# Two transformer blocks in one kernel: rotations of the woven attention cut into slices, and four copies and read-outs put elsewhere in their engines' order

## What is computed

```python
def first_block(x, mem, ...):
    ...
        h = h + memory_cross_attention(rms_norm(h, xattn_norm_g[i]), memn, w_q[i], w_k[i], w_v[i], w_xo[i])
        h = h + swiglu(rms_norm(h, ffn_norm_g[i]), w_gate[i], w_up[i], w_down[i])

def second_block(x, ...):            # two layers
        yA = forgetting_attention(heads(qA), heads(kA), heads(vA), fA, forget_bias[l])      # "fox"
        yB = dsa_attention(rope(heads(qB), pos), rope(kB, pos), vB, rope(qI), rope(kI), wI) # "dsa"
        r = retention(rope(heads(qC), pos), rope(heads(kC), pos) * HEAD_DIM ** -0.5, heads(vC))
        yC = head_groupnorm(r, ret_norm[l]) * jax.nn.silu(gC)
        yD = sliding_window_gqa(rope(heads(qD), pos), rope(heads(kD), pos), heads(vD), attn_sinks[l])  # "swa"
        branch = jnp.einsum('bsnc,ncd->bsnd', ys, w_branch[l])
        merged = jnp.sum(jax.nn.sigmoid(gates) * branch, axis=2)
        x = x + merged @ w_out[l]
        u = causal_dwconv(rmsnorm(x, ffn_norm[l]) @ w_up[l], conv_w[l], conv_b[l])
        a, b = jnp.split(u, 2, axis=-1)
        x = x + (jax.nn.silu(a) * b) @ w_down[l]
```

## Time and profile before

| | |
|---|---|
| median of three runs | 3037.11 us (3036.61 to 3038.03) |
| the profiled execution | 3039.78 us, its span 3037.8 us |
| PE busy | 2988.0 us (98%) |
| DVE, ACT, POOL busy | 1391.3, 1289.9, 1398.2 us (46%, 42%, 46%) |
| granted TensorE clock, mean | 0.997 |
| chain that ended last | PE 89%, DVE 6%, ACT 2%, POOL 1% |
| first woven attention, layer 0 and 1 | about 1085 to 1258 and 2122 to 2295 us |

### The profile page before, as it was taken

The page is one execution under the profiler, slowest core; times in us unless marked ns, Lnnn a source line. Parts: engine busy times, 40 slices in busy tenths (PEclk is TensorE's granted clock), DMA queues, the critical chain, the costliest instruction groups (busy, mean ns, idle before and its releaser), DMA issues.

```text
span 3037.8 us, 39928 instructions
## 1 busy us (share of the span) xinstructions
PE 2988.0 (98%) x15302; PEld 2438.1 (80%) x15302; DVE 1391.3 (46%) x2189; ACT 1289.9 (42%) x2219; POOL 1398.2 (46%) x1002
## 2 busy tenths in 40 slices
PE   8999999999999999999999999999999999999998
PEld 7778887788888777878888888878787788878887
DVE  7874351421113878562116433168776520264322
ACT  5443443433333446554234444244564533354432
POOL 5345574444444543234455454554332354544543
PEclk9999999999999999999999999999999999999999
DMA  5234242233333423223333333244231233333332
GB/s 158 83 112 144 87 132 91 77 97 97 99 97 85 142 69 89 53 67 87 97 93 99 94 97 99 83 109 138 68 91 42 64 98 97 97 94 97 97 97 71
DMA packets 214891, 287.61 MB, mean 95 GB/s; under 512 B 42682, under 2 KB 122610, under 8 KB 213042
## 3 DMA queue, kind: packets, MB, share of 16 engines
q1 hardware_dynamic: 212210, 279.88, 31.5%
q0 software_dynamic: 880, 2.99, 0.3%
q10 hardware_dynamic: 1616, 2.23, 0.2%
HBM read 269.80 MB, written 4.72 MB: 90 GB/s over the span
## 4 chain that ended last, share of the span: by engine, by line
PE 89%; DVE 6%; ACT 2%; POOL 1%; issue 1%; DMA 0%; ACTq 0%; SPq 0%; DVEq 0%
PE half L732 80%; PE half L1169 1%; PE half L1155 1%; PE half L1226 1%; POOL wL L2917 1%; PE half L1138 1%; PE half L1133 1%; DVE arena L2082 1%; DVE arena L2681 1%; DVE arena L2715 1%; PE half L987 0%; PE half L1004 0%; DVE rms L2073 0%; PE half L1212 0%; DVE arena L2706 0%
## 5 line engine op out<-in xcount | busy, mean ns | idle before, releaser
L2917 POOL TENSOR_TENSOR wL<-slot,wH 128x512 fp32r<-128x512 f32 (+1 forms) x976 | 1366.5, 1407 | 1610.1 <-ACT wH L1336 1609.0
L1336 ACT ACTIVATE wH<-slot 128x512 fp32r<-128x512 f32 (+1 forms) x976 | 603.4, 625 | 1229.3 <-PE half L732 1223.7
L732 PE MATMUL half<-nH,wH 128*128 128x512 f32 x2336 | 922.6, 395 | 8.1 <-POOL wL L2917 3.1
L732 PE MATMUL half<-nH,wL 128*128 128x512 f32 x2336 | 910.2, 390 | 0.0
L732 PE MATMUL half<-nL,wH 128*128 128x512 f32 x2336 | 909.7, 389 | 0.0
L732 PE MATMUL half<-arena_split,wH 128*128 128x512 f32 (+1 forms) x2432 | 735.8, 385 | 1.7 <-issue 0.8
L732 PEld LDWEIGHTS half<-nH,wH 128*128 128x128 f32 x2336 | 438.5, 188 | 119.7 <-issue 20.2
L732 PEld LDWEIGHTS half<-arena_split,wH 128*128 128x128 f32 x2432 | 451.2, 188 | 94.6 <-issue 3.4
L732 PEld LDWEIGHTS half<-nH,wL 128*128 128x128 f32 x2336 | 438.5, 188 | 92.6
L732 PEld LDWEIGHTS half<-nL,wH 128*128 128x128 f32 x2336 | 438.8, 188 | 89.2 <-issue 1.4
L732 PE MATMUL half<-arena_split,wL 128*128 128x512 f32 (+1 forms) x1216 | 466.4, 384 | 0.0
(11 more groups left out here) (351 smaller groups left out, 2656.5 us busy)
## 6 DMA issues: line engine op xcount, KB each, us to landing
slot<-in_w_in SPq DMA_DIRECT2D x344, 256.0 KB, 2.7
slot<-in_w_up SPq DMA_DIRECT2D x440, 128.0 KB, 2.2
slot<-in_w_down SPq DMA_DIRECT2D x132, 256.0 KB, 2.6
slot<-in_w_branch SPq DMA_DIRECT2D x64, 256.0 KB, 2.6
slot<-in_w_out SPq DMA_DIRECT2D x48, 256.0 KB, 2.8
slot<-in_w_gate SPq DMA_DIRECT2D x88, 128.0 KB, 2.1
arena<-arena SPq DMA_DIRECT2D x40, 256.0 KB, 4.4
slot<-in_w_proj_b SPq DMA_DIRECT2D x16, 256.0 KB, 2.9
```

The lines of the kernel that those rows point to most:

```text
L732: mm = pe.matmul(dst, lhsT, rhs, start=(k == 0 and m == 0), stop=(k == last and m == 2))
L1336: act.activation(wH[:, p, 0:cols], slot[:, s, 0:cols], ACT.Copy).then_inc(weights_high, 1)
L2917: pool.tensor_tensor(wL[:, p, 0:cols], slot[:, s, 0:cols], plainly(wH[:, p, 0:cols]), ALU.subtract)\
```

## The change

1. **Rotations.** Every rotation is cut into twelve instructions of 128x512 (`rope_slices`): four times sin, four times cos, four sums. A table says how many are done after which iteration (count in brackets): qB after -1, 0, 1, 2 (3 each); qC after 4 (1), 5 (1), 6 (2), 7 (2), 8 (1), 9 (1), 10 (2), 11 (2); kC after 13 (1), 14 (2), 15 (1), 16 (2), 17 (2), 18 (2), 20 (2); qD after 24 (2), 25 (2), 26 (2), 27 (3), 28 (3). None is left inside an iteration.
2. **Stacks.** `STACK_AT` goes from (9, 11, 17, 21) to (11, 14, 18, 22).
3. **First block, copy of the queries.** The last unit of `awq1` on PE signals after its first two banks, and ACT copies these two before it waits for the unit's end.
4. **Read-outs of gates 1 and 2.** ACT reads the first bank right after the last unit, ahead of the copy of the turn, and the other three where all four were read.
5. **Retention gate.** DVE does it in iteration 1 of `WEAVE_S` between `negated` and `inverse`, and not after `normed`.
6. **Feed-forward.** Units 4 and 5 of `bup2` are rounded by ACT around the first group's silu and rounding, and only 6 and 7 after `conv_last(1)`.

```diff
-STACK_AT = (9, 11, 17, 21)
+STACK_AT = (11, 14, 18, 22)
...
-                    unit(ps[1], "awq1", k, stream)
+                    if k < KD - 1:
+                        unit(ps[1], "awq1", k, stream)
+                    else:
+                        unit(ps[1], "awq1", k, stream, part=[0, 1]).then_inc(S["bank_done"], 1)
+                        unit(ps[1], "awq1", k, stream, part=[2, 3]).then_inc(weights_used, 1)
...
+            act.wait_ge(S["bank_done"], 1)
+            act.activation(xq[:, 4:6, :], banks(1)[:, 0:2, :], ACT.Copy).then_inc(S["xq_read"], 1)
             done(act, "awq1")
-            act.activation(xq[:, 4:6, :], banks(1)[:, 0:2, :], ACT.Copy).then_inc(S["xq_read"], 1)
...
+                    for n in (1, 2):
+                        if (f"bgt{n}a", KD - 1) in weave.at(it):
+                            done(act, f"bgt{n}a", l)
+                            if n == 1:
+                                read_out(act, "btC", l)
+                            else:
+                                act.wait_ge(S["yc_split"], l + 1)
+                            evac_by_bank(gate_b[n], jobs.half[f"bgt{n}a"], part=[0])
                     if weave.has(it):
                         turned(s, False)
...
-                    if 0 < g < NG - 1:
+                    if g == 1:
+                        round_units("bup2", l, 0, [6, 7], 512)
+                    elif 0 < g < NG - 1:
                         others(f"bup{g + 1}", l)
...
                     act.activation(conv[:, p, 0:2, :], conv[:, p, 0:2, :], ACT.Silu).then_inc(S["silu"], 1)
+                    if g == 0:
+                        round_units("bup2", l, 0, [4], 512)
                     act.wait_ge(S["ff_ready"], l * NG + g + 1)
                     round_ff(conv[:, p, 0:2, :], g)
+                    if g == 0:
+                        round_units("bup2", l, 0, [5], 512)
...
+                def rope_slices(name, buf, n, first, count):
+
+                    if first == 0:
+                        dve.wait_ge(S["partners"], l * 320 + 64 * n + 64)
+                        read_out(dve, name, l)
+                    for at in range(first, first + count):
+                        op, j = divmod(at, NB)
+                        if op == 0:
+                            link(dve.tensor_tensor(part[:, j, :], part[:, j, :], C["sin"], ALU.mult))
+                        elif op == 1:
+                            link(dve.tensor_tensor(buf[:, j, :], buf[:, j, :], C["cos"], ALU.mult))
+                        else:
+                            ins = dve.tensor_tensor(buf[:, j, :], buf[:, j, :], part[:, j, :], ALU.add)
+                            if j == NB - 1:
+                                ins.then_inc(S["roped"], 1)
...
                     if amid:
-                        rope(*amid)
+                        amid()
...
-                pieces = {0: ("bqB", qB, 1, [0]), 1: ("bqB", qB, 1, [1]), 3: ("bqB", qB, 1, [2]),
...
-                    woven(WEAVE_A, it, ("bqC", qC, 2, [0]) if it == 6 else None)
-                    if it in pieces:
-                        rope(*pieces[it])
+                    woven(WEAVE_A, it)
+                    for name, buf, n, taken in turned_by:
+                        if it in taken:
+                            rope_slices(name, buf, n, sum(taken[x] for x in taken if x < it), taken[it])
                     if it - 1 in STACK_AT:
...
-                    woven(WEAVE_S, it)
+                    woven(WEAVE_S, it, retained_gated if it == TURN_C else None)
```

More of the change, by code:

```diff
@@ L1344, in others, with evac_by_bank @@
                 round_units(name, l, i, range(SPLITS, ring.units[name]), cols)
-            def evac_by_bank(to, h, func=ACT.Copy, **kw):
-                for j in range(4):
+            def evac_by_bank(to, h, func=ACT.Copy, part=range(4), **kw):
+                for j in part:
                     ins = act.activation(to[:, j, :], ps[h][:, j * T:j * T + T], func, **kw)
@@ L1951, in gate_read @@
                         read_out(act, gates_used[n - 3], l)
-                    elif n == 1:
-                        read_out(act, "btC", l)
-                    elif n == 2:
-                        act.wait_ge(S["yc_split"], l + 1)
                     h = jobs.half[name]
                     if n < 3:
-                        evac_by_bank(gate_b[n], h)
+                        evac_by_bank(gate_b[n], h, part=range(1, 4) if n else range(4))
                     else:
@@ L2755, in _ @@
                 dve.wait_ge(S["forget_rows"], 16 * PAIRS * (l + 1))
-                pieces = {0: ("bqB", qB, 1, [0]), 1: ("bqB", qB, 1, [1]), 3: ("bqB", qB, 1, [2]),
-                          7: ("bqC", qC, 2, [1]), 9: ("bqC", qC, 2, [2]),
-                          13: ("bkC", kC, 3, [0]), 15: ("bkC", kC, 3, [1]), 17: ("bkC", kC, 3, [2]),
-                          26: ("bqD", qD, 4, [0]), 27: ("bqD", qD, 4, [1]), 28: ("bqD", qD, 4, [2])}
+                turned_by = [("bqB", qB, 1, {-1: 3, 0: 3, 1: 3, 2: 3}),
+                             ("bqC", qC, 2, {4: 1, 5: 1, 6: 2, 7: 2, 8: 1, 9: 1, 10: 2, 11: 2}),
+                             ("bkC", kC, 3, {13: 1, 14: 2, 15: 1, 16: 2, 17: 2, 18: 2, 20: 2}),
+                             ("bqD", qD, 4, {24: 2, 25: 2, 26: 2, 27: 3, 28: 3})]
                 def weigh_retained(i):
@@ L2792, in _, with retained_gated @@
                 dve.tensor_tensor(grouped, grouped, wide(mean, HD), ALU.subtract).then_inc(S["group_centred"], 1)
+                def retained_gated():
+                    dve.wait_ge(S["gc_ready"], l + 1)
+                    dve.wait_ge(S["y_turned"], l + 1)
+                    h = jobs.half["btC"]
+                    for c in range(NB):
+                        ins = dve.scalar_tensor_tensor(out=gC[:, c, :], in0=ps[h][:, c * T:c * T + T],
+                                                       scalar=vec[:, W_RET + c:W_RET + c + 1], in1=gC[:, c, :],
+                                                       op0=ALU.mult, op1=ALU.mult)
+                        if c < 3:
+                            ins.then_inc(S["bank_read"], 1)
+                    ins.then_inc(S["yc_ready"], 1)
+                    dve.wait_ge(S["yc_ready"], l + 1)
+                    dve.sem_inc(drained[h], 1)
                 for it in WEAVE_S.its:
-                    woven(WEAVE_S, it)
+                    woven(WEAVE_S, it, retained_gated if it == TURN_C else None)
                     if it == -AHEAD:
@@ L2801, in _ @@
                         dve.tensor_tensor(grouped, grouped, wide(mean, HD), ALU.mult).then_inc(S["group_normed"], 1)
-                    if it == TURN_C:
-                        dve.wait_ge(S["gc_ready"], l + 1)
-                        dve.wait_ge(S["y_turned"], l + 1)
-                        h = jobs.half["btC"]
-                        for c in range(NB):
-                            ins = dve.scalar_tensor_tensor(out=gC[:, c, :], in0=ps[h][:, c * T:c * T + T],
-                                                           scalar=vec[:, W_RET + c:W_RET + c + 1], in1=gC[:, c, :],
-                                                           op0=ALU.mult, op1=ALU.mult)
-                            if c < 3:
-                                ins.then_inc(S["bank_read"], 1)
-                        ins.then_inc(S["yc_ready"], 1)
-                        dve.wait_ge(S["yc_ready"], l + 1)
-                        dve.sem_inc(drained[h], 1)
                     if it == TURN_C + 2:
@@ L2895, in _ @@
             for k in range(4, KD):
-                dve.wait_ge(S["bank_done"], k - 3)
+                dve.wait_ge(S["bank_done"], 1 + k - 3)
                 dve.tensor_tensor(hT[:, k, :], hT[:, k, :], banks(jobs.half["bdn1"])[:, k - 4, :], ALU.add).then_inc(S["residual"], 1)
```

## The result

The changed kernel takes 3049.77 us (median of six, 3048.3 to 3052.47) against 3036.99 of before in the same comparison: ratio 1.0040, 95% interval 1.0029 to 1.0051. It is slower by 12 to 13 us. The profiled execution took 3052.47 us, its span is 3050.4, so 12.6 more than the span of before.

What follows compares the result with a forecast made beforehand. PE, busy 98% of 3037.8 us, was taken as the bound, so only its waits count. Fox and dsa steps +14.4, other parts -6.0 and clock +3.3 give +11.7 on the median 3037.1: 3048.8 us, range 3036 to 3058.

Steps and rivals of the forecast that it cites:

- scores(7): Iterations 2 to 4: three sums stand before biased(6), so PE's wait grows by 2.2 us a layer (1.3 to 3.2).
- scores(9): One slice after iteration 4 pushes biased(8) past a POOL start: +1.3 us a layer (0.2 to 1.7).
- scores(11): Two slices after iteration 6, with a POOL start falling into them: +1.6 us a layer (0.5 to 2.6).
- scores(13): One slice after iteration 8; stretched biased(12) meets a second POOL instruction: +1.2 us a layer (0.2 to 1.8).
- scores(16): PE waits for the stack rest of pair 0, now done after normed(14): +2.7 us a layer (1.7 to 2.9).
- clock: After the new long PE waits, one stretch at 1.2 GHz a layer: +3.3 us for both layers (0 to 6.8).
- other parts: Query copy, retention gate, gate 2 and bup2 unit 4 lose their PE waits: 6.0 us saved in both layers.
- three terms of 1.04: At scores(9), scores(11) and scores(13), slices make a DVE instruction meet a POOL one: 1.04 us each, 6.2 in all.
- A: Rival: at biased(6) and biased(14) sums fall into DVE's idle time, fox and dsa waits go; 3023.7 us, 6%.
- B: Rival: POOL starts move too, no 1.04 term comes, scores(16) is at 1.7, clock stays; 3037.3 us, 20%.
- C: Rival: clock falls after each of four long waits and one more, not hidden by the loop; 3056 us, 12%.
- D: The forecast itself, all terms as summed: 3048.8 us, 3043 to 3055, 60%.

Runs made afterwards that it cites:

- e9: Changed kernel with qB's three sums after iteration 3 instead of 2 and qC's first slice after 5; ratio to before 1.0001.
- e2: Changed kernel with STACK_AT back at (9, 11, 17, 21), slices kept; ratio to before 1.0052.
- e7: Changed kernel with qC's slices after odd iterations alone, 5 (2), 7 (4), 9 (2), 11 (4); ratio to before 1.0029.
- e10: Changed kernel with the bias of even fox steps made one iteration earlier, inside the even iteration; ratio to before 0.9991.
- e3: Kernel before with STACK_AT (11, 14, 18, 22) and nothing else; ratio to before 1.0015.
- e1: Changed kernel with rotations whole and stacks where they were, so parts 3 to 6 alone; ratio to before 0.9982.

## Why the prediction was right

It said 3048.8 (3036 to 3058), measured are 3049.77, and the waits are those that it named: slices and stack rest in the even loop of DVE. That it came within 1 us is luck. The clock cost 8.8 us in both layers together and not 3.3, and all other terms together made 3.8 and not 8.4; the two errors nearly cancel. By its own steps, per layer:

| step | predicted | measured | read from |
|---|---|---|---|
| scores(7) | +2.2 | +1.9 | wait 3.07 against 1.15; e9 takes it back |
| scores(9) | +1.3 | 0 | hidden behind the low clock; 1.04 in layer 1 of e2 |
| scores(11) | +1.6 | +1.4 | wait 1.42; gone in e7 and e10 |
| scores(13) | +1.2 | +1.35, +1.27 | wait 1.35 and 1.27; gone in e7 and e10 |
| scores(15) | -1.2 | -1.6 | 1.88 to 0.27 |
| scores(16) | +2.7 | +2.75, +2.6 | e3 has it without slices |
| scores(31) | -0.6 | -0.6 | column 32 |
| clock | +1.65 | +4.4 | 3.0 behind scores(7), 1.4 behind scores(16) |
| other parts, both layers together | -6.0 | -6.8, in e1 -6.0 | the columns to 0 and to the end, in part by the start |

**Duration of a slice.** 0.70 was taken; the slices alone took 0.68 or 0.69, and in after 1.65 to 1.78 where POOL had started before them. Scores(7) shows both. DVE and POOL after the change, the stretch of the earlier trace rows:

```profile
1124.61 4.08 DVE L2621 TENSOR_TENSOR arena<-arena 128x512 f32<-128x512 f32 x3
1128.61 1.14 DVE L2712 SCALAR_TENSOR_TENSOR arena<-consts,ftm,arena 128x384 f32<-128x384 f32 x2
...
1123.13 4.40 POOL L2951 TENSOR_TENSOR wL<-slot,wH 128x512 fp32r<-128x512 f32 x3 [7.21 <-ACT wH L1340]
```

The sums took 4.08, not 2.1, but biased(6) behind them 1.14, not 3.22: the slices took over the stretching, and the term came out right without my having seen that. A meeting cost a slice 1.1 us; 1.04 was taken.

**What DVE pays beside POOL.** The three terms of 1.04 were the least certain. At scores(11) it came about as told (biased(10) took 2.06, against 1.14 before). At scores(13) the price came but from another instruction: biased(12) took 2.45 as before, and it was normed(10) that took 1.84 where 0.75 would do, beside the POOL instruction at 1159.65. At scores(9) it did not come: biased(8) took 1.41, as before. So a start in some tenths can't be forecast, only that with more in the queue one more meeting is likely; e1 shows that even the kernel before had one by a hair. The Trainium skill (SBUF — State Buffer, Who interferes with whom) calls it an exclusive lock for the whole instruction. The traces agree: of the 96 slices in after, 81 took 0.68 or 0.69 us, and the other 15 had started while a POOL instruction ran. Each of these 15 ended 0.55 us after that instruction did. In the ten kernels with slices that holds of 121 of 122 such slices, whether they took 0.70 us or 1.79. A slice that only shared with POOL would not end at a fixed distance from POOL's end.

**Scores(16).** This was right in place and size, and the wait comes without the slices too (e3). It is the length of the way from normed(14) through the rest. Where one of the two meets a POOL instruction it is 2.6 to 2.75 (normed took 1.84 in layer 0 of after, the rest 2.33 in e3 and e9 and 2.34 in e10); where both do, as in e7 (1.74 and 2.35), it is 4.04.

**Clock.** This is the term that was mis-sized: +1.65 a layer, measured +4.4. I allowed one stretch a layer and said that behind scores(7) a slower PE would be hidden by PE's further waits on DVE. There were two a layer. From scores(7) to (15), +4.13 less the waits (1.42 + 1.35 + 0.27 - 1.88) leaves 3.0; from (16) to (20) it is 1.4. The stretch at scores(7) was twice as long, 6.83 us, and it was not hidden: scores(8), 5.23 us behind scores(7) in before, came 8.13 behind. It only swallowed the term at scores(9). The two errors, +2.75 and -1.3, leave 1.45 a layer; the smaller terms of the steps take about half of it back, and the other parts 0.4.

**The other parts.** All four did what the sum says: 1.1 for the query copy, 0.8 and 0.24 for the gates, and 1.3 rather than 1.4 for bup2 (unit 4's wait is now 0.29). e1, which has them alone, gains 6.0 in their columns.

**A sum.** The low bounds, as they are listed, add up to 1.9 a layer and not to 2.6, which makes some 3034 and not 3035; the range given, from 3036, was not taken from it.

**Rivals.** A (slices fit, faster) is refuted by the eight waits. B (waits move and balance) is too: the waits did not move, they were added. Of the three terms of 1.04 only that at scores(9) stayed away, scores(16) was at 2.6 to 2.75 and not at 1.7, and the clock fell. C (the clock falls after each of the four long waits, and the loop does not hide it) came true for the clock: it cost 5.5 us more than in my sum. Its total of 3056 did not come, since the other terms were 4.6 lower. So the number is that of D, and the clock that of C.

**Left open.** Why the low clock behind scores(7) behind the same wait of 3.07 was 6.83 us long in both layers of after and one of e2, and 3.41 in the other of e2 and both of e7, was not settled. The traces do show this: the five stretches of 6.83 us all began while PE still waited, 0.48 to 1.30 us before the wait ended, and the three of 3.41 us behind a wait of 3.07 began 0.44 to 0.63 us after its end. But three of 3.41 us at waits of 2.6 also began before the end, by 0.43 to 0.51 us, so the start alone does not decide it.

## What to carry to other kernels

An engine that is busy 46% of the time can still be on the path. Find the loop that ends at the bound engine's wait, and ask of each instruction in the queue if it stands behind the event the loop waits for (then all of it is paid) or ahead of it (then it is free up to the idle time there). Cutting an operation into pieces adds places where it can stand in the way, and each must be priced with what else stands there, DMAs behind its end included; taking the bias out of the loop gave 15 us by the ratios (e10), and the best placing of slices with the same stacks 12 (e9). Where two engines exclude each other, add one meeting's price as a likely cost and don't trust tenths of a microsecond.

## What the runs showed of the hardware

**Low clock after waits.** Over the twelve profiled kernels, two layers each, I counted PE's waits of 1 us and more between 100 and 3010 us, and whether a stretch of clock 0.50 came with each: of 24 waits of 2.59 us and more, 23; of six of 1.87 to 1.97, two; of 24 of 1.68 (all at the same place, L732 <- DVE nL), 11; of 36 shorter ones, one. The stretches are 3.41 or 6.83 us long. One of 3.41 costs 1.2 to 1.5 us where PE has work behind it. After the wait of 1.68 it costs little: PE is busy 1.3 us longer, but otherwise soon waits 0.81 for POOL. There the same kernel can have it in one layer and not in the other (e1 has it in layer 1 alone). So in after the wait of 3.07 us was paid as 6, that of 2.75 as 4.2, and shortening the first to 1.90 (e10) gave more than the difference.

**DVE and POOL.** A 128x512 tensor_tensor on DVE with both sources in SBUF took 0.68 us alone and 1.78 where POOL's had started just before it, and it then ended 0.55 us after POOL's. POOL's own took 1.25 to 1.34 alone (most 1.29), and up to 1.75 where such a slice was first. With starts 0.03 us apart in the records it went either way.
